# The scan's 64x64 products on four tiles of TensorE instead of two, in a hybrid attention and RWKV-7 encoder

## The chip, the cores and the metric

The kernel runs on one core of a Trainium2 chip. The metric is the device time of one execution in microseconds. The kernel before took 3055.45 us, the median of three runs (3053.56 to 3060.9).

## The reference

One encoder layer is applied to two sequences, of 1024 and 256 tokens, with model width 1024. The layer normalises the tokens, projects them once, and sends the columns to two groups of heads:

- four heads of differential attention (width 512), and
- eight heads of bidirectional RWKV-7 time mixing (width 512, head size 64).

Both results are joined, projected by `w_out` and added to the input. Then come 16 SwiGLU experts that each choose their tokens, and a last norm. The part that matters here is the time mixing. For each head, and once in each direction of time, it runs

```
def step(S, inp):
    r_t, w_t, k_t, v_t, a_t, b_t = inp
    Sa = jnp.einsum('bhij,bhj->bhi', S, a_t)
    S = S * w_t[:, :, None, :] + Sa[..., None] * b_t[:, :, None, :] + v_t[..., None] * k_t[:, :, None, :]
    y = jnp.einsum('bhij,bhj->bhi', S, r_t)
    return S, y
...
y = ys[0] + ys[1]
mean = jnp.mean(y, axis=-1, keepdims=True)
var = jnp.mean((y - mean) ** 2, axis=-1, keepdims=True)
y = ((y - mean) * lax.rsqrt(var + GN_EPS)).reshape(B, T, RWKV_WIDTH) * lnx_w + lnx_b
...
return ((y + bonus) * g)
```

with a state S of 64x64 per head. Everything is fp32 at the interface.

## The kernel before, in words

The kernel is a row of blocks, each closed before the next one opens: norm and projection, attention, the scan, the group norm of the scan's result, the output projection with the router, the experts, the last norm. Features go between blocks through the DRAM tensor `feat` (40 tiles of 128 x 1280).

**The scan** (L754 to L1150) works in chunks of C = 64 tokens. One step g takes 128 tokens, two chunks, of all eight heads and of both directions d (direction 1 runs from the end). There are NG = 10 steps, eight for the long sequence and two for the short one. Two heads lie in one tile of 128 partitions, head 0 of the pair on partitions 0 to 63 and head 1 on 64 to 127, and there are RT = 4 such tiles f. An array for a step has NI = 8 items i (4 tiles by 2 chunks) of 64 columns. All products are 64x64 times 64x32, 64x64 or 64x128 in fp32.

PE's work is written out by hand, and each group ends with a semaphore. `heads(out, lhsT, rhs)` (L895 to L898) issues two products, one for each partition half: rows 0 to 63 into output partitions 0 to 63, rows 64 to 127 into 64 to 127. These are the diagonal tiles of the 128x128 array. `turned` (L900 to L903) transposes in the same way, by a product with the identity. PSUM has eight banks of 512 columns; direction d owns four of them, `at_bank(d, b, i)` with b from 0 to 3.

A step of PE is, in this order:

1. *pairs*: `bt` and then `kt` against `ar`, 128 columns each, for both directions, into banks 0/1 and 2/3.
2. the first transpose, of `invT`, into bank 0.
3. *levels* l = 1 to 5, which double the size of the block in which a triangular matrix is inverted. Each level has `ax` for both directions (bank 0), then at levels 2 to 4 the transposes of one of three token arrays for both directions (bank 3, the table TOKENS), then `xax` for both directions: up to two calls per item, into banks 1 and 2.
4. the *scan half* c = 0 and 1: G (bank 3), u (bank 0), and y with the state's update (banks 1 and 2), for both directions each.

The other engines follow by semaphores. ACT copies PSUM to SBUF after each group (L998, L1002, L1006, L1011, L1014) and computes the decays of the next step behind c = 0. DVE masks the pairs (L1078, L1081, L1069), adds each level's result to `inv` and `invT` (L1094, L1096), and adds y and the state (L1109 to L1123). Between these it does the next step's preparation: `rates` after levels 2 to 4 (L1042 to L1048), `running` before the y of c = 0 (L1033, L1035), and `blocks` before the y of c = 1 (L1056 to L1061). Each of these stands at a fixed place in DVE's program. POOL multiplies the masked pairs with the ten level masks of a step (L883), level 1 of both directions first, then levels 2 to 5 of direction 0, then those of direction 1. PE waits for each of them with `lvl_masked`.

The block behind the scan loads `bonus`, `gate` and `w_out` (L1183 to L1188), sums heads with a matrix of ones (L1206), and norms and gates the result `yacc`. ACT and POOL meanwhile split `w_out` into two halves of 16 bits.

Lines that the prediction names beside these: L1576 is a product of the experts in f16, on the full array.

Of the kernel before, what the change touches and what calls it, by code (L numbers as in the profile page):

```python
# [8 lines left out]
P = 128  # L9
D = 1024  # L10
KD = D // P
# [5 lines left out]
RW = 512  # L17
RT = RW // P
# [4 lines left out]
C = 64  # L23
# [30 lines left out]
def build(nc, tokens, gains, sub_g, w_in, lam_qk, par, w2, a2, g2, w_out, w_router,  # L54
# [12 lines left out]
    with ExitStack() as ctx:  # L67
# [785 lines left out]
        with nc.Block() as block:  # L853
# [33 lines left out]
            @block.tensor  # L887
            def _(pe):
                H = (slice(0, C), slice(C, 2 * C))

                def at_bank(d, b, i, w=C):
                    o = (4 * d + b) * 512 + i * w
                    return ps[:, o:o + w]

                def heads(out, lhsT, rhs, start=True, stop=True):  # L895
                    for h in H:
                        ins = pe.matmul(out[h], lhsT[h], rhs[h], start=start, stop=stop)  # L897
                    return ins  # L898

                def turned(out, lhsT):  # L900
                    for h in H:
                        ins = pe.matmul(out[h], lhsT[h], ident[h, h], start=True, stop=True)
                    return ins  # L903

                def step(g):
                    par = g % 2
                    for b, x in ((0, bt), (2, kt)):
                        for d in range(2):
                            if b == 0:
                                pe.wait_ge(bd_ready[d], g + 1)  # L910
                                if g:
                                    pe.wait_ge(y_read[d], 2 * g)
                            for i in range(NI):
                                ins = heads(at_bank(d, b + i // 4, i % 4, 2 * C), x[d][:, i],
                                            ar[d][par][:, i].rearrange("p a b -> p (a b)"))
                            ins.then_inc(pairs_psum[d], 1)
                    for d in range(2):
                        pe.wait_ge(masks_ready[d], 3 * g + 2)
                        for i in range(NI):
                            ins = turned(at_bank(d, 0, i), invT[d][:, i])  # L920
                        ins.then_inc(first_psum[d], 1)
                    for l in range(1, NL + 1):
                        for d in range(2):
                            pe.wait_ge(inv_ready[d], NL * g + l)
                            pe.wait_ge(lvl_masked[d], NL * g + l)
                            for i in range(NI):
                                ins = heads(packed(at_bank(d, 0, i, C // 2), l), alv[d][:, l - 1, i],
                                            half_of(inv[d][:, i], l, d == 1))
                            ins.then_inc(ax_psum[d], 1)
                        for dt, q in TOKENS.get(l, ()):  # L930
                            if q == 0:
                                pe.wait_ge(masks_ready[dt], 3 * g + 3)
                                pe.wait_ge(vb_in[dt], 16 * g + 16)
                            else:
                                pe.wait_ge(tok_read[dt], NTOK * g + q)
                            x = (vb, bt, kt)[q][dt]
                            for i in range(NI):
                                ins = turned(at_bank(dt, 3, i), x[:, i])
                            ins.then_inc(tok_psum[dt], 1)
                        for d in range(2):  # L940
                            pe.wait_ge(prod_ready[d], NPR * g + l)
                            if l == 1:
                                pe.wait_ge(masks_ready[d], 3 * g + 3)
                            for i in range(NI):
                                x = prod(d, l)[:, i]
                                if l < NL:
                                    heads(packed(at_bank(d, 1, i, C // 2), l), invT[d][:, i], half_of(x, l, d == 1))
                                ins = heads(packed(at_bank(d, 2, i, C // 2), l), x, half_of(invT[d][:, i], l, d == 0))
                            ins.then_inc(xax_psum[d], 1)
                    for c in range(2):  # L950
                        for d in range(2):
                            pe.wait_ge(state_ready[d], 2 * g + c + 1)
                            if c == 0:
                                pe.wait_ge(tok_read[d], NTOK * (g + 1))
                            for f in range(RT):
                                i = 2 * f + place(d, c)
                                heads(at_bank(d, 3, f), ar[d][par][:, i, 0], state[d][:, f], stop=False)
                                ins = heads(at_bank(d, 3, f), km[d][:, i, 0], tokv[d][:, i], start=False)
                            ins.then_inc(g_psum[d], 1)
                        for d in range(2):  # L960
                            pe.wait_ge(prod_ready[d], NPR * g + NL + 2 * c + 1)
                            if c == 0:
                                pe.wait_ge(invT_final[d], g + 1)
                            for f in range(RT):
                                ins = heads(at_bank(d, 0, f), invT[d][:, 2 * f + place(d, c)], gu[d][:, f])
# [12 lines left out]

                for g in range(NG):
                    step(g)  # L980
# [45 lines left out]
            def _(v):  # L1026
# [47 lines left out]
                def step(g):  # L1074
                    more = g + 1 < NG
                    for d in range(2):
                        v.wait_ge(pairs_psum[d], 2 * g + 1)
                        v.tensor_tensor(inv[d], pair_banks(d, 0).rearrange("p (a w b) -> p a w b", w=2, b=C)[:, :, 0],  # L1078
                                        lvl[:, d, 0:1, :].broadcast_to([P, NI, C]), ALU.mult)
                        v.drain()  # L1080
                        v.tensor_tensor(invT[d], inv[d], ident2[:, :].unsqueeze(1).broadcast_to([P, NI, C]),  # L1081
                                        ALU.add)
                        v.drain().then_inc(masks_ready[d], 1)
                    for d in range(2):
                        mask_pairs(d, bm, 0)
                    for d in range(2):
                        v.wait_ge(pairs_psum[d], 2 * g + 2)
# [92 lines left out]
        with nc.Block() as block:  # L1180
            @block.sync
            def _(sp):
                sp.dma_start(bonus, feat[F_BONUS:F_BONUS + RT].rearrange("t p n -> p t n")).then_inc(post_in, 16)  # L1183
                sp.dma_start(gate, feat[F_GATE:F_GATE + RT].rearrange("t p n -> p t n")).then_inc(post_in, 16)

                sp.dma_start(wo_raw, w_out.rearrange("(k p) n -> p k n", p=P)).then_inc(wo_in, 16)
                sp.dma_start(wr, w_router.rearrange("(k p) n -> p k n", p=P)).then_inc(wo_in, 16)
                sp.dma_start(g2n, gains[1:2, :].partition_broadcast(P)).then_inc(wo_in, 16)  # L1188
                for b in range(2):
# [1 line left out]

            @block.gpsimd
            def _(pool):
                pool.wait_ge(post_in, 32)
# [23 lines left out]
            def _(act):  # L1218
                for f in range(RT):
# [6 lines left out]
                                   scale=1.0 / 64).then_inc(std_ready, 1)  # L1226

                    if f == 0:
                        act.wait_ge(wo_in, 48)
# [8 lines left out]
            def _(v):  # L1238
# [5 lines left out]
                                           ALU.mult, ALU.add).then_inc(centred, 1)  # L1244

                centre(0)
                v.wait_ge(post_in, 32)
                for f in range(RT):
                    if f + 1 < RT:
                        centre(f + 1)  # L1250
# [43 lines left out]
        with nc.Block() as block:  # L1294
# [33 lines left out]
            @block.tensor  # L1328
            def _(pe):
                pe.drain().then_inc(out_psum, 2)  # L1330
                pe.wait_ge(wo_in, 48)

                def project(t, b, half):
                    for k in range(KD):
# [78 lines left out]
            def _(v):  # L1413
                for b in range(2):
                    v.drain().then_inc(h6_stored[b], 16)
                v.wait_ge(wo_in, 48)
# [444 lines left out]
```

## Time and profile before

| | |
|---|---|
| median of three runs | 3055.45 us |
| profiled execution, its own time | 3056.16 us |
| its span, first to last instruction | 3054.3 us |
| PE busy over the span | 2750.1 us (90%) |
| weight loads (PEld) | 2130.6 us (70%) |
| DVE | 1995.9 us (65%) |
| ACT | 1438.8 us (47%) |
| POOL | 321.0 us (11%) |
| the scan's stretch, 743 to 1325 us | 582.0 us |
| PE busy in it | 573.9 us |

An engine's busy time is the time in which at least one of its instructions is in work, so overlapping products on PE count once. PEld is the same engine loading weights beside its products. A share over the whole span is an average over blocks with different limits; the scan is best read by itself. In a timeline a row is a run of instructions of one line, with its start, its length, its count and the idle time before it.

### The profile page before, as it was taken

The page shows a single profiled execution, that of the slowest core. Times are in us where ns is not written, and L with a number is a line of the kernel's source. Part 1 is how long each engine was busy: PE and PEld are TensorE (multiplying, and loading weights), DVE is VectorE, ACT ScalarE, POOL GpSimd, SP SyncE. Part 2 cuts the span into 40 slices and gives each one's busy share as a digit, 9 for nine tenths or more (in the row PEclk, how much of TensorE's full clock was granted, in tenths as well). Part 3 has the DMA queues.
Part 4 walks back from the last instruction along what each step waited for, and adds up shares of the span by engine and source line. Part 5 has one row for each costly group of instructions (what it writes and reads, how often), then busy time and mean ns, then how long its engine had stood idle before and what let it go on. Part 6 is the DMA issues. An engine that isn't in the chain of part 4 may idle for free. (4 is left out here: it accounts for less than half of the span.)

```text
span 3054.3 us, 90989 instructions
## 1 busy us (share of the span) xinstructions
PE 2750.1 (90%) x39070; PEld 2130.6 (70%) x39070; DVE 1995.9 (65%) x3188; ACT 1438.8 (47%) x2171; POOL 321.0 (11%) x260
## 2 busy tenths in 40 slices
PE   5999988996999999955934999999999999999994
PEld 3455544665999999942524777888877777788872
DVE  3344077776565455434268888888888888888883
ACT  3211155664222222222223666666666666666663
POOL 0000000002113112213200100111111000011000
PEclk8999999997999999977966999999999999999997
DMA  4113141002112112033315999999999999999984
GB/s 129 34 37 142 27 193 67 0 0 77 52 51 74 52 45 80 11 147 110 124 41 203 308 307 333 312 311 318 309 316 308 309 300 314 320 319 309 315 278 154
DMA packets 282900, 544.78 MB, mean 178 GB/s; under 512 B 13296, under 2 KB 96880, under 8 KB 282576
## 3 DMA queue, kind: packets, MB, share of 16 engines
q1 hardware_dynamic: 273728, 505.62, 48.1%
q0 software_dynamic: 8848, 34.08, 4.3%
q8 instruction: 296, 4.85, 0.6%
q14 instruction: 28, 0.23, 0.0%
HBM read 487.23 MB, written 52.43 MB: 177 GB/s over the span
## 5 line engine op out<-in xcount | busy, mean ns | idle before, releaser
L1677 DVE SCALAR_TENSOR_TENSOR arena<-arena 128x1024 f16<-128x1024 f32 x768 | 904.2, 1221 | 95.2 <-ACT arena L1622 95.0
L1576 PE MATMUL ps<-arena 128*128 128x160 f16 x12288 | 854.4, 233 | 8.2 <-DVE arena L1686 3.3
L1576 PEld LDWEIGHTS ps<-arena 128*128 128x128 f16 x12288 | 850.8, 98 | 12.8 <-issue 9.6
L1622 ACT ACTIVATE arena<-arena 128x1024 f16<-128x1024 f32 x768 | 766.7, 1049 | 145.3 <-PE ps L1601 144.9
L897 PE MATMUL ps<-arena 64*64 64x32 f32 (+2 forms) x14080 | 501.5, 224 | 22.4 <-DVEq L1062 21.2
L897 PEld LDWEIGHTS ps<-arena 64*64 64x64 f32 x14080 | 481.5, 135 | 28.5 <-DVEq L1062 21.4
L1593 PE MATMUL ps<-arena 128*128 128x512 f16 x1536 | 363.6, 388 | 0.0
L389 PE MATMUL ps<-arena 128*128 128x512 f16 (+1 forms) x1584 | 285.7, 344 | 0.7 <-ACT arena L235 0.7
L1593 PEld LDWEIGHTS ps<-arena 128*128 128x128 f16 x1536 | 142.3, 99 | 182.8 <-issue 36.4
L389 PEld LDWEIGHTS ps<-arena 128*128 128x128 f16 x1584 | 154.9, 98 | 131.7 <-ACT arena L235 1.2
L1643 ACT ACTIVATE arena<-ps 128x160 f32<-128x160 f32 x256 | 77.7, 304 | 256.8 <-PE ps L1576 256.6
L883 POOL TENSOR_TENSOR arena<-arena,lvl 128x512 f32<-128x512 f32 x100 | 123.8, 1273 | 429.8 <-DVEq L1072 429.1
L1094 DVE TENSOR_TENSOR arena<-arena,ps 128x256 f32<-128x256 f32 x80 | 33.8, 422 | 184.8 <-PE ps L897 184.8
L307 DVE SCALAR_TENSOR_TENSOR arena<-arena 128x1024 f16<-128x1024 f32 x22 | 26.9, 1225 | 181.2 <-ACT arena L240 181.2
L600 PE MATMUL ps<-arena 128*128 x288 | 126.1, 582 | 17.6 <-DVEq L695 15.3
L1705 DVE SCALAR_TENSOR_TENSOR arena<-ps,arena 128x160 f32<-128x160 f32 x256 | 82.5, 322 | 79.1 <-ACT arena L1643 77.6
L1002 ACT COPY arena<-ps 128x256 f32<-128x256 f32 x100 | 37.7, 377 | 203.7 <-PE ps L897 203.7
L1336 PE MATMUL ps<-arena 128*128 128x512 f16 x480 | 109.4, 386 | 24.2 <-POOL arena L1326 24.2
L240 ACT ACTIVATE arena<-arena 128x1024 f16<-128x1024 f32 x22 | 23.1, 1056 | 217.5 <-PE ps L389 217.5
L1528 POOL TENSOR_TENSOR carry<-carry 1x1 f32<-1x1 f32 x16 | 2.9, 183 | 1127.1 <-ACT arena L1660 1127.1
L651 ACT ACTIVATE arena<-arena 128x1024 f32<-128x1024 f32 (+1 forms) x80 | 81.6, 1021 | 64.0 <-DVE arena L710 63.1
L1601 PEld LDWEIGHTS ps<-arena 128*32 128x32 f16 x3072 | 70.2, 96 | 55.4 <-issue 54.2
(219 smaller groups left out, 2911.0 us busy)
## 6 DMA issues: line engine op xcount, KB each, us to landing
arena<-w_gate SPq DMA_DIRECT2D x128, 1024.0 KB, 5.1
arena<-w_up SPq DMA_DIRECT2D x128, 1024.0 KB, 5.6
arena<-w_down SPq DMA_DIRECT2D x128, 1024.0 KB, 6.5
arena<-feat SPq DMA_DIRECT2D x120, 256.0 KB, 4.7
feat<-arena SPq DMA_DIRECT2D x20, 640.0 KB, 3.0
arena<-w_in SPq DMA_DIRECT2D x21, 512.0 KB, 3.9
arena<-tokens SPq DMA_DIRECT2D x20, 512.0 KB, 4.1
feat<-arena POOLq DMA_DIRECT2D x1, 7680.0 KB, 22.8
```

What stands on the lines that cost most here:

```text
L389: ins = pe.matmul(ps[:, b * 2048 + o:b * 2048 + o + c], wb2[:, b, w, k * P:(k + 1) * P], hT2[:, x, k, o:o + c], start=(k == 0 and n == 0), ...
L600: ins = pe.matmul(ps[:, m * T0 + o:m * T0 + o + w], qz[:, m, t0 + i * P:t0 + (i + 1) * P], qk[:, ds(h + HEADS_A, 1), t0 + o:t0 + o + w] .r ...
L651: act.activation(sc[:, u % 2, m, 0:n], sc[:, u % 2, m, 0:n], ACT.Exp, bias=srow[:, u % NR, m:m + 1], accum_out=srow[:, u % NR, 2 + m:3 + m ...
L883: pool.tensor_tensor(alv[d][:, l - 1], bm[d][:, :, 0], lvl[:, d, l:l + 1, :].broadcast_to([P, NI, C]), ALU.mult).then_inc(lvl_masked[d], 1)
L897: ins = pe.matmul(out[h], lhsT[h], rhs[h], start=start, stop=stop)
L1336: ins = pe.matmul(bank(2 * b + half), ot2[:, b, x, k], wo2[:, k, w, half * 512:(half + 1) * 512], start=(k == 0 and n == 0), stop=(k == KD ...
L1576: ins = pe.matmul(ps[:, o:o + SLOTS], part(4 * c + 2 * w + k // 4, pw) [:, k % 4, f * P:(f + 1) * P], xT2[:, px, k], start=(k == 0 and i = ...
L1593: pe.matmul(bank(2 + half), hid2[:, px, n, 0:CAP0], part(k, pw)[:, f, half * 512:(half + 1) * 512], start=first, stop=last)
L1622: act.activation(split[k % SPLIT][:, q * PW:(q + 1) * PW], ring[k % RING][:, q * PW:(q + 1) * PW], ACT.Copy, scale=W_SCALE).then_inc(w_hi, 1)
L1643: act.activation(sil[:, n % 2], ps[:, (n % 2) * 512:(n % 2) * 512 + SLOTS], ACT.Silu, scale=1.0 / W_SCALE).then_inc(silu_ready, 1)
L1677: v.scalar_tensor_tensor(split[k % SPLIT][:, WCH + q * PW:WCH + (q + 1) * PW], ring[k % RING][:, q * PW:(q + 1) * PW], W_SCALE, split[k % ...
L1705: v.scalar_tensor_tensor(h32[:, n % 2], ps[:, (n % 2) * 512 + SLOTS:(n % 2) * 512 + 2 * SLOTS], 1.0 / W_SCALE, sil[:, n % 2], ALU.mult, AL ...
```

## The change

Two new helpers issue the two products of a call on the other two tiles of the array: rows 0 to 63 into output partitions 64 to 127, and rows 64 to 127 into 0 to 63.

- The first transpose, all `ax`, the first call of each `xax` item (levels 1 to 4), all of G and u, and three of the five calls of y use the crossed helpers. The others stay on the diagonal.
- At levels 2 to 4 the token transposes alternate call by call with `ax` of the same level, instead of following both directions. Which direction and array a level has is unchanged. Their waits now stand ahead of the `ax` group that they alternate with.
- In y the two kinds alternate: crossed, diagonal, crossed, diagonal, crossed.
- What is written crossed lies on exchanged partition halves: `invT` (filled by two half operations of DVE instead of one), `gu` between G and u, and `yacc`. In DVE's program bm's mask for a direction now follows that direction's `invT` directly.
- Because `yacc` is exchanged, `bonus` and `gate` are loaded in halves that are exchanged (four DMAs of 64 partitions instead of two of 128), the rows of `w_out` that meet it too (three DMAs instead of one), and the two norm parameters are rolled on the host by 64.

```diff
+                def across(out, lhsT, rhs, start=True, stop=True):
+                    for h in range(2):
+                        ins = pe.matmul(out[H[1 - h]], lhsT[H[h]], rhs[H[h]], start=start, stop=stop)
+                    return ins
+
+                def turned_across(out, lhsT):
+                    for h in range(2):
+                        ins = pe.matmul(out[H[1 - h]], lhsT[H[h]], ident[H[h], H[h]], start=True, stop=True)
+                    return ins
...
-                            ins = turned(at_bank(d, 0, i), invT[d][:, i])
+                            ins = turned_across(at_bank(d, 0, i), invT[d][:, i])
...
+                            turn = TOKENS[l][d] if l in TOKENS else None
+                            if turn is not None:
+                                dt, q = turn
+                                if q == 0:
+                                    pe.wait_ge(masks_ready[dt], 3 * g + 3)
+                                    pe.wait_ge(vb_in[dt], 16 * g + 16)
+                                else:
+                                    pe.wait_ge(tok_read[dt], NTOK * g + q)
+                                x = (vb, bt, kt)[q][dt]
                             for i in range(NI):
-                                ins = heads(packed(at_bank(d, 0, i, C // 2), l), alv[d][:, l - 1, i],
-                                            half_of(inv[d][:, i], l, d == 1))
-                            ins.then_inc(ax_psum[d], 1)
-                        for dt, q in TOKENS.get(l, ()):
-                            ...
-                            for i in range(NI):
-                                ins = turned(at_bank(dt, 3, i), x[:, i])
-                            ins.then_inc(tok_psum[dt], 1)
+                                ins = across(packed(at_bank(d, 0, i, C // 2), l), alv[d][:, l - 1, i],
+                                             half_of(inv[d][:, i], l, d == 1))
+                                if i == NI - 1:
+                                    ins.then_inc(ax_psum[d], 1)
+                                if turn is not None:
+                                    ins = turned(at_bank(dt, 3, i), x[:, i])
+                            if turn is not None:
+                                ins.then_inc(tok_psum[dt], 1)
...
-                                    heads(packed(at_bank(d, 1, i, C // 2), l), invT[d][:, i], half_of(x, l, d == 1))
+                                    across(packed(at_bank(d, 1, i, C // 2), l), invT[d][:, i], half_of(x, l, d == 1))
                                 ins = heads(packed(at_bank(d, 2, i, C // 2), l), x, half_of(invT[d][:, i], l, d == 0))
...
-                                heads(at_bank(d, 1, f), state[d][:, f], ar[d][par][:, i, 1], stop=False)
-                                heads(at_bank(d, 1, f), tokv[d][:, i], km[d][:, i, 1], start=False, stop=False)
+                                across(at_bank(d, 1, f), state[d][:, f], ar[d][par][:, i, 1], stop=False)
                                 if f == 0:
                                     pe.wait_ge(prod_ready[d], NPR * g + NL + 2 * c + 2)
-                                heads(at_bank(d, 1, f), gu[d][:, f], bm[d][:, i, 1], start=False)
                                 heads(at_bank(d, 2, f), tokb[d][:, i], gu[d][:, f], stop=False)
-                                ins = heads(at_bank(d, 2, f), tokk[d][:, i], tokv[d][:, i], start=False)
+                                across(at_bank(d, 1, f), tokv[d][:, i], km[d][:, i, 1], start=False, stop=False)
+                                heads(at_bank(d, 2, f), tokk[d][:, i], tokv[d][:, i], start=False)
+                                ins = across(at_bank(d, 1, f), gu[d][:, f], bm[d][:, i, 1], start=False)
...
-                        v.tensor_tensor(invT[d], inv[d], ident2[:, :].unsqueeze(1).broadcast_to([P, NI, C]),
-                                        ALU.add)
+                        for h in range(2):
+                            src, dst = slice(C * h, C * h + C), slice(C - C * h, 2 * C - C * h)
+                            v.tensor_tensor(invT[d][dst], inv[d][src],
+                                            ident2[src, :].unsqueeze(1).broadcast_to([C, NI, C]), ALU.add)
                         v.drain().then_inc(masks_ready[d], 1)
-                    for d in range(2):
                         mask_pairs(d, bm, 0)
...
-                sp.dma_start(bonus, feat[F_BONUS:F_BONUS + RT].rearrange("t p n -> p t n")).then_inc(post_in, 16)
-                sp.dma_start(gate, feat[F_GATE:F_GATE + RT].rearrange("t p n -> p t n")).then_inc(post_in, 16)
-
-                sp.dma_start(wo_raw, w_out.rearrange("(k p) n -> p k n", p=P)).then_inc(wo_in, 16)
+                for h in range(2):
+                    src, dst = slice(C * h, C * h + C), slice(C - C * h, 2 * C - C * h)
+                    for x, t in ((bonus, F_BONUS), (gate, F_GATE)):
+                        sp.dma_start(x[dst], feat[t:t + RT, src].rearrange("t p n -> p t n")).then_inc(post_in, 16)
+
+                w_rows = w_out.rearrange("(k p) n -> p k n", p=P)
+                sp.dma_start(wo_raw[:, 0:RT], w_rows[:, 0:RT]).then_inc(wo_in, 16)
+                for h in range(2):
+                    src, dst = slice(C * h, C * h + C), slice(C - C * h, 2 * C - C * h)
+                    sp.dma_start(wo_raw[dst, RT:KD], w_rows[src, RT:KD]).then_inc(wo_in, 16)
```

G and u change `heads` to `across` in the same way. The waits for `post_in` go from 32 to 64 and those for `wo_in` from 48 to 80.

## Rows read from the trace of the kernel before

**Rows 1.** The page's head.
```profile
span 3054.3 us, 90989 instructions
```
**Rows 2.** Windows: stretch, length, each engine's busy time and count, clock, DMA.
```profile
743.00:1325.00 582.00, 573.88 (x17920) 566.26 (x17920) 312.32 (x585) 146.39 (x332) 123.79 (x100) 0.99 0.20 53
1325.00:1420.00 95.00, 33.00 (x67) 14.43 (x68) 50.62 (x16) 27.56 (x25) 34.48 (x16) 0.66 0.41 154
1330.00:1340.00 10.00, 6.01 (x12) 2.80 (x12) 0.00 (x0) 3.24 (x3) 0.00 (x0) 0.83 1.02 418
```
**Rows 3.** Groups by line, 743 to 1325: busy us, mean ns, idle before.
```profile
L897 PE MATMUL ps<-arena 64*64 64x32 f32 (+2 forms) x14080 | 501.5, 224 | 22.4 <-DVEq L1062 21.2 <-issue 0.7
L897 PEld LDWEIGHTS ps<-arena 64*64 64x64 f32 x14080 | 481.5, 135 | 28.5 <-DVEq L1062 21.4 <-issue 1.6
```
**Rows 4.** Waits, 743 to 1325: total us, times, longest.
```profile
DVE arena L1094 <- PE ps L897: 184.8, 80, 6.4
```
**Rows 5.** Line 1078: duration ns, first and last start us.
```profile
L1078 DVE TENSOR_TENSOR arena<-ps,lvl x20: 691/692/692, 747.1 to 1269.8; 128x512 f32<-128x512 f32 x20
```
**Rows 6.** Timeline of weight loads in one step: start, length, line.
```profile
878.07 5.88 PEld L897 LDWEIGHTS ps<-arena 64*64 64x64 f32 x192
883.82 2.00 PEld L902 LDWEIGHTS ps<-ident,arena 64*64 64x64 f32 x64
...
901.12 0.20 PEld L897 LDWEIGHTS ps<-state,arena 64*64 64x64 f32 x4
...
904.14 0.20 PEld L897 LDWEIGHTS ps<-arena,state 64*64 64x64 f32 x4
...
904.72 0.20 PEld L897 LDWEIGHTS ps<-arena,state 64*64 64x64 f32 x4
```
**Rows 7.** Timeline of DVE in the same step.
```profile
861.69 0.69 DVE L1078 TENSOR_TENSOR arena<-ps,lvl 128x512 f32<-128x512 f32 x1 [0.40 <-PE ps L897]
862.46 0.69 DVE L1081 TENSOR_TENSOR arena<-arena,ident 128x512 f32<-128x512 f32 x1
863.43 0.69 DVE L1078 TENSOR_TENSOR arena<-ps,lvl 128x512 f32<-128x512 f32 x1 [0.28 <-PE ps L897]
...
865.02 5.26 DVE L1069 TENSOR_TENSOR arena<-ps,causal 128x1024 f32<-128x1024 f32 x4
...
880.18 0.42 DVE L1094 TENSOR_TENSOR arena<-arena,ps 128x256 f32<-128x256 f32 x1 [4.99 <-PE ps L897]
...
882.05 0.42 DVE L1094 TENSOR_TENSOR arena<-arena,ps 128x256 f32<-128x256 f32 x1 [0.30 <-PE ps L897]
...
906.74 0.14 DVE L1109 COPY carry<-carry 1x1 f32<-1x1 f32 x1 [0.94 <-PE ps L897]
...
907.66 0.43 DVE L1123 TENSOR_TENSOR state<-state,eb 128x256 f32<-128x256 f32 x1
...
910.79 0.69 DVE L1056 SCALAR_TENSOR_TENSOR arena<-arena 128x512 f32<-128x512 f32 x1
911.40 0.68 DVE L1057 TENSOR_TENSOR arena<-arena 128x512 f32<-128x512 f32 x1
...
916.21 0.14 DVE L1109 COPY carry<-carry 1x1 f32<-1x1 f32 x1 [0.21 <-issue]
...
919.52 0.69 DVE L1078 TENSOR_TENSOR arena<-ps,lvl 128x512 f32<-128x512 f32 x1 [0.41 <-PE ps L897]
```
**Rows 8.** Window of line 1206 alone: PE, then PEld.
```profile
1325.30:1327.80 2.50, 2.39 (x6) 1.06 (x6) 1.00 0.58 102
```
**Rows 9.** Timeline of POOL in the same step.
```profile
866.35 12.45 POOL L883 TENSOR_TENSOR arena<-arena,lvl 128x512 f32<-128x512 f32 x10 [44.89 <-DVEq L1072]
```
**Rows 10.** Timeline behind the scan: DVE's wait for the loads.
```profile
1340.92 1.49 DVE L1243 SCALAR_TENSOR_TENSOR arena<-ps,arena 128x1280 f32<-128x1280 f32 x1 [11.60 <-DMA arena<-feat]
```
**Rows 11.** The page's costliest groups, in f16 on the full array.
```profile
L1576 PE MATMUL ps<-arena 128*128 128x160 f16 x12288 | 854.4, 233 | 8.2 <-DVE arena L1686 3.3
L1576 PEld LDWEIGHTS ps<-arena 128*128 128x128 f16 x12288 | 850.8, 98 | 12.8 <-issue 9.6
```

More of the change, by code:

```diff
@@ L925, in step @@
                             pe.wait_ge(lvl_masked[d], NL * g + l)
-                            for i in range(NI):
-                                ins = heads(packed(at_bank(d, 0, i, C // 2), l), alv[d][:, l - 1, i],
-                                            half_of(inv[d][:, i], l, d == 1))
-                            ins.then_inc(ax_psum[d], 1)
-                        for dt, q in TOKENS.get(l, ()):
[L931 to L936, printed above, removed]
-                            for i in range(NI):
-                                ins = turned(at_bank(dt, 3, i), x[:, i])
-                            ins.then_inc(tok_psum[dt], 1)
+                            turn = TOKENS[l][d] if l in TOKENS else None
[7 more added lines that the diff above has]
+                                x = (vb, bt, kt)[q][dt]
+                            for i in range(NI):
+                                ins = across(packed(at_bank(d, 0, i, C // 2), l), alv[d][:, l - 1, i],
[6 more added lines that the diff above has]
+                                ins.then_inc(tok_psum[dt], 1)
                         for d in range(2):
@@ L956, in step @@
                                 i = 2 * f + place(d, c)
-                                heads(at_bank(d, 3, f), ar[d][par][:, i, 0], state[d][:, f], stop=False)
-                                ins = heads(at_bank(d, 3, f), km[d][:, i, 0], tokv[d][:, i], start=False)
+                                across(at_bank(d, 3, f), ar[d][par][:, i, 0], state[d][:, f], stop=False)
+                                ins = across(at_bank(d, 3, f), km[d][:, i, 0], tokv[d][:, i], start=False)
                             ins.then_inc(g_psum[d], 1)
@@ L964, in step @@
                             for f in range(RT):
-                                ins = heads(at_bank(d, 0, f), invT[d][:, 2 * f + place(d, c)], gu[d][:, f])
+                                ins = across(at_bank(d, 0, f), invT[d][:, 2 * f + place(d, c)], gu[d][:, f])
                             ins.then_inc(u_psum[d], 1)
@@ L1193, in _ @@
             def _(pool):
-                pool.wait_ge(post_in, 32)
+                pool.wait_ge(post_in, 64)
                 for f in range(RT):
@@ L1228, in _ @@
                     if f == 0:
-                        act.wait_ge(wo_in, 48)
+                        act.wait_ge(wo_in, 80)
                     for k in (2 * f, 2 * f + 1):
@@ L1246, in _ @@
                 centre(0)
-                v.wait_ge(post_in, 32)
+                v.wait_ge(post_in, 64)
                 for f in range(RT):
@@ L1330, in _ @@
                 pe.drain().then_inc(out_psum, 2)
-                pe.wait_ge(wo_in, 48)
+                pe.wait_ge(wo_in, 80)
                 def project(t, b, half):
@@ L1415, in _ @@
                     v.drain().then_inc(h6_stored[b], 16)
-                v.wait_ge(wo_in, 48)
+                v.wait_ge(wo_in, 80)
                 with v.Fori(0, NTT // 2) as j:
@@ L1836 @@
     par = np.concatenate([tiles(x["shift_mu"][0], ZT)] + [tiles(x[k][0], RT) for k in ("w0", "a0")]
-                         + [tiles(x[k][0].reshape(1, RW), RT) for k in ("k_k", "k_a", "r_k", "lnx_w", "lnx_b")], axis=1)
+                         + [tiles(x[k][0].reshape(1, RW), RT) for k in ("k_k", "k_a", "r_k")]
+                         + [np.roll(tiles(x[k][0].reshape(1, RW), RT), C, axis=0) for k in ("lnx_w", "lnx_b")], axis=1)
     dist = np.abs(np.arange(P)[:, None] - (np.arange(BIAS_W)[None, :] - (T0 - P))).astype(np.float32)
```

## The prediction, made before the changed kernel was run

> **What bounds the kernel now.** I read the page's head first, then the busy time by stage: of the span of 3054.3 us [rows 1] the scan takes 582.0 us, with PE busy for 573.9 of it and DVE for 312.3, and the stage behind it, where the loads are re-cut, is the 95 us from 1325 on [rows 2]. Stages are closed blocks, so what the scan loses or gains moves the end one for one. Then the groups of the scan: the top one is PE at one helper line with 64x64 products in fp32 [rows 3]. The waits say that DVE waits for PE at one line alone for 184.8 us [rows 4], where PE itself is idle only 582.0-573.9 = 8 us [rows 2]. So PE's pace is the bound, at first.
>
> Below, a call is one `heads` or `across`: two products, one per partition half. Each product has two load and two matmul records, so a call is four of each. A step g takes, from first to last L1078 and less the 1.7 us between its two directions, (1269.8-747.1-1.7)/9 = 57.9 us [rows 5].
>
> Price of a call. In y, five calls per tile of 64x64 on 64 columns take 904.72-904.14 = 0.58 us: 117 ns each. In the levels, 192 load records (48 calls of 32 columns) take 883.82-878.07 = 5.75 us, 120 ns each, short idle included [rows 6]. Half the columns, same pace. With 128 columns, eight calls (L1078 of both directions, 863.43-861.69) take 1.74 us, 218 ns each [rows 7]. The full array in fp32 takes 2.39 us for 1280 columns, 1.87 ns a column [rows 8]; 16 products of 128 columns in 1.74 us are 0.85. So the two diagonal tiles already run side by side, and up to 64 columns a call costs 117 ns whatever its columns: two passes of 58.5 on the same pair of tiles.
>
> **The change, part by part.**
> *Alternation.* `across` uses rows h and columns 1-h, the two idle tiles. Calls that follow each other on different pairs can overlap; two on the same pair can't. Per step and at 117 ns or below there are 416 calls: 16 first transposes, 80 A·X (`ax`), 48 token transposes, 144 in `xax`, 128 in the scan half. Alternating afterwards are ax with tokens (levels 2 to 4, 96), xax levels 1 to 4 (128), and y (80, per f A H A H A, so four changes and one repeat). Not alternating: first transposes, ax at levels 1 and 5, xax at 5, all of G and u (112). No row shows two column tiles on the same rows. Bounds: 58.5 ns (all four tiles free) and 117 ns (nothing overlaps). I take 65: the second pass of a call must wait for its first, 58.5, and the next call starts with it, 6 ns for issue; it is near the low end because the two tiles that [rows 7, 8] do show lose nothing to each other. Blocks of 16 alternating calls: 1.04 us (before 1.87). One f of y: 4·65+117 = 377 ns (before 585). PE's work per step falls by 224·52+16·208 = 15 us. Most of the question is how much of that the others let through.
>
> *What is late next*, followed through the step whose L1078 is at 861.69 [rows 7].
> Head: invT becomes two instructions of half the partitions; L1078 to L1081 is 0.77 us, and a 128x512 operation of DVE without a drain behind it steps by 0.61 (910.79 to 911.40 [rows 7]). A half-partition form has no row; I price it as the whole one (bounds 0.3 and 0.7 each). Also bm's mask of direction 0 moves before direction 1's L1078. Direction 0: 862.46+0.61+0.81 = 863.88, mask ends 865.2. Direction 1: L1078 865.2, invT 865.97, mask 867.39, ready 868.72; before it was ready at 865.02+1.32+1.33 = 867.67. So the transpose of direction 1 starts 1.05 us late, at 868.72. Level 1's ax is 1.8 us as before and ends 871.5; xax gains: 2.1 us, ends 873.6 (before 874.2).
> POOL: its ten masks run 12.45 us back to back from 866.35 [rows 9], 1.24 apart. Level 2 of direction 1 is the seventh, ready at 875.13 now, and PE's block starts there at 875.28, so POOL is just hidden. POOL's second mask waits for direction 1's bm, so the seventh comes at 868.72+7.43 = 876.15, where PE could start at 874.7. New wait: 1.45 us.
> Levels 2 to 5: from the last product of a `xax` to L1094 are 0.27 us, to inv_ready 1.1. DVE then does a `rates` operation (L1042) for the next step: L1094 of direction 0 is at 880.18, that of direction 1 at 882.05 after 0.30 idle [rows 7]. It can't take direction 1 before 1.6 us after direction 0, so direction 1's inverse is ready 0.27+1.6+0.83 = 2.7 us after direction 0's xax ends, against 1.04 us of PE work there. A level is then 2.7+1.04+1.04 = 4.8 us (before 7.6; 0.06 is a seam). With xax 2 of direction 0 ending at 878.2, level 4's ends at 887.7, level 5 (2.7 and three blocks of 0.93, not alternating: 5.5) ends at 893.2. Before: G's first load at 901.12 [rows 6]. Saved up to there: 7.95 us.
> Scan half: G, u and ACT's two copies between are unchanged (3.0 us for c=0). y: 1.5 instead of 2.3 us, twice. DVE's `running` for the next step moves along with them. State of c=0 d=1 is ready 1.7 us behind y, at 900.95 (before just ahead of `blocks`, 910.79). Then DVE does `blocks`, 910.79 to 916.21 = 5.42 us [rows 7], and only then adds y of c=1; the next step's first products wait for y_read, 0.9 us behind L1109 (906.74 to 907.66 [rows 7]): 900.95+5.42+0.9 = 907.3. PE's y would be done at 906.1, so DVE takes 1.2 us of what PE gains. Before: 917.56 (2.0 ahead of the next L1078, 919.52 [rows 7]).
> A step saves 917.56-907.3 = 10.2 us, of 15 that PE's work falls by. The last step has no `blocks`: 11 us. Nine and one: 103 us. The step followed is as long as the mean (L1078 at 861.69 and 919.52, 57.8 beside 57.9 us [rows 7, 5]), so it stands for the others.
>
> *A page against it.* The Trainium skill (TensorE: Matmul & The Clock Gate, Part 3: Packing small matmuls) says a weight load overlaps matmuls in flight only when the row group differs. This case's trace speaks against the strict form: L1576's loads (850.8 us) and matmuls (854.4 us) of full 128 rows share the same stretch [rows 11]. By that rule an alternating call would gain nothing, and the sum would be the second rival below. The same section says, and the page TensorEngine Tiling (Array Packing), Key Properties, repeats, that distinct tiles load and multiply in parallel; no row here has such a pair.
>
> *Loads behind the scan.* bonus and gate come in four issues of 64 partitions instead of two, w_out in three instead of one; bytes are equal. SP's issues are 0.4 to 1.4 us and lie under the transfers; DVE waits for them until 1340.92, 11.6 us [rows 10]. At equal rate: 0. If halves of the partitions landed at half the rate, 15.5 us more (the block opens at 1325.4, they land at 1340.9). I take 0: the bytes set the time, as 418 GB/s on a full DMA share shows there [rows 2]. Rolled parameters, the swapped halves of yacc and the waits 64 and 80 cost nothing on the device.
>
> **Sum.** 3054.3-103 = 2951 us span; the run's own time is 1.9 above the span (3056.2), which gives 2953; the profiled run is 0.7 above the median of 3055.45, so 2952. With 58.5 ns a call: 0.2 us less at levels 2, 3 and 4 and 0.2 less in y, level 1 hidden under POOL: 8 us less, 2944.
>
> **Rivals.**
> 1. Half overlap: the two tiles on the same rows share a feed, a call costs about 90 ns. Blocks are 1.44 us. Level 1's loss stays under POOL; level 2's xax 0 ends 0.9 later, a level is 2.7+2.9 = 5.6 (0.8 more, twice), y is 0.4 longer, twice. A step saves 10.2-0.9-1.6-0.8 = 6.9 us: 2986 us. For it: a floor of 58.5 ns that isn't columns could be a load port. Against: the two tiles that run together now show no such sharing.
> 2. No overlap: the change doesn't do what it says, 117 ns stays. Left are +1.05 us of DVE head and about -0.35 from ax d1 no longer waiting at levels 2 to 4 (tokens lie between): +0.7·10 = 7 us, 3062, within noise.
> 3. Changing pairs costs, the other side: at each change the next tile's weight load can't hide. Its price is up to one load record, 135 ns [rows 3]; some 286 changes a step. If the exposed part is a third of it, 45 ns, that is 12.9+0.7 us a step: 3191 us. It turns slower than before by over 0.3% once a change exposes more than 1 ns on top of rival 2. For: the floor is set by loads. Against: loads of the next product already start under the matmuls, 850.8 beside 854.4 us [rows 11].
> 4. The clock: PE now idles 1.0, 1.45 and about three times 0.6 us a step and 1.2 at its end. The granted clock is 0.99 in the scan and 0.66 in the stage with PE busy 33 of 95 us [rows 2]. PE would be busy near 88%; if a tenth of the scan ran at half clock, +25 us: 2977, inside the range.
>
> **How the numbers follow.** Forecast 0.70 (with rival 4 in it), half overlap 0.09, none 0.11, costly change 0.10. 2952 is the likeliest; its own range is 2930 to 2985. The range for 8 in 10 takes in half overlap and an overlap worse than half: 2928 to 3008. Faster by over 0.3% (9 us, what a measurement of this kernel can tell): 0.80; within: 0.09; slower: 0.11 (costly change, and the loads at half rate on top of rival 2).
>
> **What would show it.** Right: L1078 to L1078 near 47 us; y's five calls in 0.38 us and an alternating block of 16 in 1.04; POOL as releaser of PE at level 2; DVE's idle before L1094 nearly gone; PE waiting for DVE at the step's end. G and u unchanged. DVE's L1243 wait still near 11.6 us. Wrong: blocks of 1.87 us (rival 2), longer (rival 3), steps below 44 us (DVE's half-partition operations or its chain cheaper than read), or the 95 us behind the scan longer.

## The result, and the profile after

The changed kernel takes 3087.1 us, the median of five runs (3080.0 to 3095.0), against 3055.45 us before. The ratio is 1.010, 95% interval 1.0075 to 1.0125: slower by 1%, where 3.4% faster was forecast. Its profiled execution took 3086.4 us.

Three marks cut both traces: the first masking operation of DVE in the scan (L1078, now L1092), the first product of the group norm behind it (L1206, now L1227), and the first product of the output projection (L1336, now L1357).

| us | before | after | forecast |
|---|---|---|---|
| scan, mark 1 to 2 | 578.3 | 585.3 | 475 |
| block behind it, mark 2 to 3 | 87.7 | 105.3 | 87.7 |
| all that follows | 1641.2 | 1647.0 | 1641.2 |

The last row is scatter: the same stretch takes 1644.3 us in e2 and 1649.6 in e4 below, which leave scan and experts as they were. The other two rows are the result.

The page of the kernel after: its span, the products' busy time, and the queue that carries instructions (packets, MB, share).
```profile
span 3084.5 us, 91013 instructions
PE 2651.0 (86%) x39070; PEld 2016.8 (65%) x39070; DVE 2013.2 (65%) x3208; ACT 1432.7 (46%) x2171; POOL 320.8 (10%) x260
q8 instruction: 296, 4.85, 0.6%
```
PE is busy 99 us less for the same 39070 matmul records, and the kernel is slower. So the tiles do overlap, and PE then stands idle. Windows of the kernel after answer [rows 2]: the scan, one alternating `xax` block of 64 matmul records, one idle stretch, and one block of 32 that does not alternate.
```profile
743.00:1332.00 589.00, 470.38 (x17920) 450.61 (x17920) 327.60 (x605) 140.58 (x332) 123.85 (x100) 0.89 0.20 52
869.30:870.23 0.93, 0.93 (x66) 0.93 (x65) 0.76 (x2) 0.00 (x0) 0.93 (x2) 1.00 0.00 0
871.10:873.00 1.90, 0.32 (x23) 0.21 (x13) 0.15 (x1) 0.37 (x1) 1.90 (x3) 1.00 0.00 0
909.26:910.20 0.94, 0.94 (x32) 0.94 (x34) 0.91 (x2) 0.10 (x1) 0.00 (x0) 1.00 0.00 0
```
Sixteen alternating calls take 0.93 us, 58 ns each, as the forecast's low end had it; eight that stay on one pair take 0.94, 117 ns each. The granted clock of the whole scan is 0.89, not 0.99. The waits of the kernel after, from 743 to 1360 us (total, times, longest), answer [rows 4]:
```profile
DVE arena L1109 <- PE ps L897: 168.2, 61, 6.4
PE ps L902 <- issue: 43.3, 37, 2.2
PE ps L897 <- issue: 27.8, 23, 2.0
PE ps L912 <- DVEq L1086: 17.6, 10, 1.9
PE ps L907 <- issue: 13.0, 12, 1.6
```
"Issue" is time in which PE waited for nothing that the profile shows; before it was under 2 us in the scan (0.7 in [rows 3]). PE's wait for DVE's mask at L1086 was forecast at 1.0 us a step; it is 1.8. In levels 2 to 4 the idle stretches come at one distance, whatever group they fall in. Three windows of PE there, each from one resumption to the next:
```profile
873.00:876.92 3.92, 2.29 (x127) 1.00 0.46 125
876.92:880.81 3.89, 2.30 (x127) 1.00 0.07 17
880.81:884.63 3.82, 2.15 (x128) 1.00 0.02 4
```
128 matmul records, with 128 loads 256 instructions, and then a pause until 3.8 to 3.9 us are over. The queue q8 moves 4.85 MB in 296 packets, 16 KB each; over 256 instructions that would be 64 bytes each. So the reading was: PE's program arrives in packets of 64 products, one per 3.85 us or so when PE is always hungry. A step has 1792 records, 14.0 packets, 53.9 us.

The queue's own rows bear this out. Of q8 the scan has (packets, MB, share), 743 to 1332 us:
```profile
q8 instruction: 140, 2.29, 1.6%
```
That is 14.0 packets a step. The three packets that began at 870.38, 874.34 and 878.05 us had landed at 871.76, 875.49 and 879.48; PE resumed at 873.01, 876.94 and 880.83, each time 1.25 to 1.45 us later. Over the scan, 61 of PE's 96 idle stretches of over 0.3 us end 1.2 to 1.55 us behind the landing of such a packet. The kernel before has the same 140 packets there, and its PE idles 8 us in all.

The step itself: DVE's line of mask operations answers [rows 5], and its timeline [rows 7].
```profile
L1092 DVE TENSOR_TENSOR arena<-ps,lvl x20: 691/692/693, 746.9 to 1278.0; 128x512 f32<-128x512 f32 x20
```
```profile
857.57 0.69 DVE L1092 TENSOR_TENSOR arena<-ps,lvl 128x512 f32<-128x512 f32 x1 [0.17 <-PE ps L897]
858.35 1.39 DVE L1097 TENSOR_TENSOR arena<-arena,ident 64x512 f32<-64x512 f32 x2
859.85 1.23 DVE L1083 TENSOR_TENSOR arena<-ps,causal 128x1024 f32<-128x1024 f32 x1
861.20 0.69 DVE L1092 TENSOR_TENSOR arena<-ps,lvl 128x512 f32<-128x512 f32 x1
861.97 1.73 DVE L1097 TENSOR_TENSOR arena<-arena,ident 64x512 f32<-64x512 f32 x2
863.82 3.91 DVE L1083 TENSOR_TENSOR arena<-ps,causal 128x1024 f32<-128x1024 f32 x3
```
(1278.0-746.9-3.6)/9 = 58.6 us a step, against 57.9; 3.6 us lie between the masks of the two directions. bm's mask of direction 1 starts 6.25 us behind L1092; 5.70 was forecast.

The block behind the scan answers [rows 2, 10]: one window (busy times, clock, DMA share, GB/s) and DVE's wait.
```profile
1350.00:1360.00 10.00, 0.00 (x0) 0.00 (x0) 0.00 (x0) 0.00 (x0) 0.00 (x0) 0.50 1.03 200
```
```profile
1360.81 1.49 DVE L1264 SCALAR_TENSOR_TENSOR arena<-ps,arena 128x1280 f32<-128x1280 f32 x1 [24.73 <-DMA arena<-feat]
```
The DMA engines are fully busy as before, at 200 GB/s instead of 418.

### The profile page after: what moved, and what is told of

It is laid out like the page before. It is cut to its first block and busy times, and to the rows that moved or that the text cites. A ratio compares the mean times of both kernels' runs of the same rounds, so it can differ in the third digit from the quotient of the medians.

```text
span 3084.5 us, 91013 instructions
## 1 busy us (share of the span) xinstructions
PE 2651.0 (86%) x39070; PEld 2016.8 (65%) x39070; DVE 2013.2 (65%) x3208; ACT 1432.7 (46%) x2171; POOL 320.8 (10%) x260
## 3 DMA queue, kind: packets, MB, share of 16 engines
q8 instruction: 296, 4.85, 0.6%
## 5 line engine op out<-in xcount | busy, mean ns | idle before, releaser
L902 PE MATMUL ps<-arena 64*64 64x32 f32 (+1 forms) x8320 | 352.6, 234 | 44.9 <-issue 43.3
L902 PEld LDWEIGHTS ps<-arena 64*64 64x64 f32 x8320 | 324.8, 152 | 52.9 <-issue 47.4
L897 PE MATMUL ps<-arena 64*64 64x32 f32 (+2 forms) x5760 | 263.5, 244 | 59.0 <-issue 27.8
L897 PEld LDWEIGHTS ps<-arena 64*64 64x64 f32 x5760 | 244.0, 146 | 63.7 <-issue 42.1
L600 PE MATMUL ps<-arena 128*128 x288 | 126.1, 582 | 17.6 <-DVEq L695 15.3
L1357 PE MATMUL ps<-arena 128*128 128x512 f16 x480 | 109.1, 385 | 23.7 <-POOL arena L1347 23.7
```

Source lines behind the costliest of these rows:

```text
L600: ins = pe.matmul(ps[:, m * T0 + o:m * T0 + o + w], qz[:, m, t0 + i * P:t0 + (i + 1) * P], qk[:, ds(h + HEADS_A, 1), t0 + o:t0 + o + w] .r ...
L902: ins = pe.matmul(out[H[1 - h]], lhsT[H[h]], rhs[H[h]], start=start, stop=stop)
L1357: ins = pe.matmul(bank(2 * b + half), ot2[:, b, x, k], wo2[:, k, w, half * 512:(half + 1) * 512], start=(k == 0 and n == 0), stop=(k == KD ...
```

## The experiments

Nine kernels ran. Scan and block are between the marks of the table above; the ratios of medians are against the kernel before on the same chip. e3, e4, e5 and e7 ran once: their totals have no interval, and what rests on them is read from their traces.

### The loads: e1_whole_loads and e2_half_loads_before

```
e1, from the kernel after (same for gate; w_out in one piece; waits 32 and 48)
- for h in range(2): ... sp.dma_start(x[dst], feat[t:t + RT, src]...)
+ sp.dma_start(bonus, feat[F_BONUS:F_BONUS + RT].rearrange("t p n -> p t n"))
e2, from the kernel before: the halved loads, with dst = src
```


> The changed kernel with bonus, gate and w_out loaded whole, as before (so the halves of the gated result and of w_out's rows are not exchanged, and the output differs). Theory A, loads of half the partitions are slow and make the block behind the scan longer: DVE's wait for the loads falls from 24.7 back to 11.6 us, first project product 88 us behind the scan's end instead of 105, total near 3070. Theory B, the block is longer for another reason (clock, ACT's order): total stays near 3087.

> The kernel before with only the loads of bonus, gate and w_out cut into halves of 64 partitions, each into its own half, nothing exchanged. If halves are the cost: +13 to +17 us, near 3070. If the exchange of halves (source rows of one half into the partitions of the other) is the cost: 3055 to 3057, no change.

Measured: e1 3072.0 us (ratio 1.0058, 1.0041 to 1.0075), block 86.5 us, scan 587.6. e2 3074.6 us (1.0063, 1.0046 to 1.008), block 105.1, scan 577.9. DVE's waits for the loads, e1 from the waits and e2 from the timeline, and a window of e2:
```profile
DVE arena L1258 <- DMA arena<-feat: 11.8, 1, 11.8
```
```profile
1351.44 1.49 DVE L1249 SCALAR_TENSOR_TENSOR arena<-ps,arena 128x1280 f32<-128x1280 f32 x1 [24.83 <-DMA arena<-feat]
```
```profile
1335.00:1345.00 10.00, 0.49 (x3) 0.08 (x1) 0.00 (x0) 0.00 (x0) 0.00 (x0) 0.79 1.03 206
```
The halves are the cost, not the exchange: loads into 64 partitions run at half the rate even with nothing exchanged. It is the whole of the 17.6 us. DVE's wait is 13 us of it. The block's length goes by ACT, whose first step on `w_out` waits for `w_out` and for the small loads queued behind it, `gains` last; it starts 46.1 us behind mark 2 in the kernel after (1378.26) and 27.9 before (1353.26).

### The supply of instructions: e4_pace and e3_fewer_transposes

e4 is the kernel before with a block of its own between scan and group norm; `same` is a diagonal call, `cross` a crossed one, each call into the next of the eight banks. A drain stands between the parts.
```
+ for n in range(160):
+     same(n, 64)
...
+ for n in range(160):
+     (cross if n % 2 else same)(n, 64)
...
+ for n in range(96):
+     (cross if n % 2 else same)(n, 128)
...
+ with pe.Fori(0, 20) as j:
+     for n in range(8): (cross if n % 2 else same)(n, 64)
```


> The kernel before with a block of PE alone between scan and group norm, no waits on others: 160 calls of 64 columns on the diagonal, 160 alternating, 96 alternating of 128 columns, and 160 alternating of 64 columns as a loop of 20 by 8 calls. Theory A (supply of 3.85 us for 32 calls): 18.7, then 17 to 20 with gaps of 1.9 us every 128 matmul records, then 10.5 to 11.5; the loop is 9.3 if its instructions stay on the engine and 18 or more if they are fetched again. Theory B (the gaps need DVE's and ACT's waits): 18.7, 9.3, 10.5, 9.3.

The four parts, and below them three resumptions of the second part (PE alone):
```profile
1321.80:1340.50 18.70, 18.66 (x639) 18.69 (x640) 0.00 (x0) 0.00 (x0) 0.00 (x0) 1.00 0.02 5
1340.80:1358.20 17.40, 10.26 (x627) 9.59 (x628) 0.00 (x0) 0.00 (x0) 0.00 (x0) 1.00 0.02 4
1358.50:1370.00 11.50, 11.23 (x390) 10.38 (x383) 0.00 (x0) 0.00 (x0) 0.00 (x0) 1.00 0.02 4
1370.50:1381.70 11.20, 11.15 (x639) 11.04 (x640) 0.00 (x0) 0.00 (x0) 0.00 (x0) 1.00 0.01 1
```
```profile
1343.16:1346.91 3.75, 2.09 (x128) 1.00 0.02 4
1346.91:1350.65 3.74, 2.09 (x128) 1.00 0.02 4
1350.65:1354.67 4.02, 2.09 (x128) 1.00 0.01 4
```
The same 160 alternating calls take 17.4 us as straight code, idle for 7.1 of them, and 11.2 us as a loop of 8 calls, with no idle stretch. Nothing else waits or is waited for in this block. Only where the instructions come from differs, so the pauses are instruction supply; theory B falls. The queue agrees (q8 in the second part, then in the loop, each for 1280 instructions):
```profile
q8 instruction: 4, 0.07, 1.5%
q8 instruction: 1, 0.02, 0.5%
```
(The second part's fifth packet began 0.4 us ahead of the window.) All five pauses of the second part end 1.3 to 1.5 us behind the landing of a packet. The diagonal calls, 18.7 us for 5 packets, already ran at the supply's pace: in its calls of up to 64 columns the kernel before had no slack that four tiles could use. (The loop's 70 ns a call, above 58, was not followed up.)

e3 takes instructions out of the changed kernel: only the last of eight token transposes is issued, and ACT writes zeros for the tokens.
```
- if turn is not None:
+ if turn is not None and i == NI - 1:
```


> The changed kernel with one token transpose of eight at each place (84 of 832 products a step are left out) and ACT writing zeros for the tokens. Theory A, PE waits for its instructions, which come in packets of 16 KB (64 products in fp32) at 3.85 us each: 1.3 packets less a step, 5 us, the scan 50 us shorter, 3037. Theory B, the gaps come from the four tiles or from DVE's chain: the alternating transposes cost next to nothing, the scan is 0 to 10 us shorter, 3077 or above.

Measured: the scan 568.7 us, 16.6 shorter; 3128.6 us in all, since what follows the block took 1708 us (its tokens are zero; why that is slower was not followed up). In number it lies between the theories. The window shows what the forecast left out:
```profile
740.00:1313.00 573.00, 520.92 (x16240) 509.53 (x16240) 329.74 (x606) 140.65 (x332) 123.88 (x100) 0.76 0.20 53
```
The granted clock was 0.76, against 0.89. A step of e3 had 10 to 38 us at the low clock. A line through its nine step lengths against those times gives 50.9 us at full clock; the same through the 18 steps of the changed kernel and e1 gives 54.9 us, and 0.28 us more for each us at the low clock (correlation 0.84). So 4.0 us less for 1.31 packets, 3.1 a packet, on a fit (3.85 were expected); e4 is the clean proof.

### The clock: e7_idle_diagonal and e5_filled

e7 is the kernel before, diagonal tiles only, with PE made to wait.
```
+ if l < NL:
+     v.tensor_copy(km[d], km[d])
  v.drain().then_inc(inv_ready[d] if l < NL else invT_final[d], 1)
```


> The kernel before, diagonal tiles only, with one more DVE operation (km copied onto itself, 1024 columns, 0.6 to 1.2 us) ahead of each direction's inv_ready at levels 1 to 4, so that PE waits for DVE there: 3 to 8 us of PE idle a step in pieces of 1 us, and no gap of supply. If idle PE alone makes the clock fall, low stretches of 3.4 us and more appear in most steps and the scan's clock falls under 0.97. If the four tiles or the 1.8 us gaps are needed, the clock stays 0.99 and steps grow by the idle time alone.

e5 is e1 with work that nobody reads put into each `xax` group.
```
+ def fill(d):
+     across(ps[:, 4 * d * 512 + 256:4 * d * 512 + 512], ident2, restart[:, 0:256])
...
  x = prod(d, l)[:, i]
+ if i in (1, 4, 6):
+     fill(d)
```


> The run with whole loads (e1_whole_loads), and in each of the ten xax groups of a step three more crossed calls of 256 columns into columns of PSUM that nobody reads: 0.43 us of PE work each in 8 instructions, so 240 instructions a step more. If PE's idle stretches are what makes the granted clock fall in the scan, the clock there rises from 0.88 towards 0.97 and the low stretches (10 to 20 us a step) fall under 5 us; supply then sets the step at about 15 packets by 3.85 = 58 us, even from step to step. If the clock falls for another reason (four tiles at work), it stays near 0.88 or falls, and steps grow to 62 us or more.

The scan of e7, then that of e1 and that of e5:
```profile
743.00:1415.00 672.00, 637.67 (x17885) 628.28 (x17884) 362.14 (x659) 146.36 (x332) 132.78 (x100) 0.89 0.17 45
```
```profile
740.00:1331.00 591.00, 481.70 (x17920) 461.52 (x17920) 327.18 (x606) 140.52 (x332) 123.91 (x100) 0.87 0.20 52
```
```profile
743.00:1358.00 615.00, 535.77 (x19120) 491.49 (x19120) 327.99 (x605) 140.66 (x332) 123.87 (x100) 0.98 0.19 50
```
PE's new wait in e7 (total, times, longest):
```profile
PE ps L897 <- DVEq L1099: 26.3, 38, 0.8
```
e7: PE idles 3.5 us a step instead of 0.7, in pieces of at most 0.8 us, and the clock falls to 0.89, with 10 to 17 us a step at 1.2 GHz where the kernel before had 3.4 us in nine steps; a step is 65 to 68 us. So neither four tiles nor supply gaps are needed for the fall: waits for DVE bring it too. A line through e7's nine steps gives 60.7 us at full clock and 0.45 us more for each us at the low clock. e5: with work in the gaps the clock is back at 0.98 (low stretches in three of nine steps), and steps are 60 to 63 us; 58 was expected, so filling cost 3 us more than its packets.

How much PE idles does not decide the clock by itself. PE still idles about 8 us a step in e5 and 1 to 5 in v2 below, both at 0.98, and 3.5 in e7 at 0.89; e3 idles 3 to 8 us at 0.76. The filling calls are also of 256 columns among calls of 32, so e5 changed more than the gaps. What made the difference stays open.

### DVE's head: e6_split_invT_before

```
- v.tensor_tensor(invT[d], inv[d], ident2[:, :].unsqueeze(1)..., ALU.add)
+ for h in range(2):
+     half = slice(C * h, C * h + C)
+     v.tensor_tensor(invT[d][half], inv[d][half], ident2[half, :].unsqueeze(1)..., ALU.add)
  v.drain().then_inc(masks_ready[d], 1)
- for d in range(2):
  mask_pairs(d, bm, 0)
```


> The kernel before with invT filled by two half operations of DVE (nothing exchanged) and bm's mask of a direction right behind it, as the change has it. By the prediction's working the transpose of direction 1 starts 1.05 us later in each step, +10 us, 3067; if half operations are no cheaper than read off the changed kernel (bm's mask of direction 1 is 6.25 us behind L1078 there, 5.70 forecast) +1.6 us a step, 3073. If the later start is caught up inside the step, as POOL's and DVE's waits there have slack, no change.

Measured: 3073.7 us (1.0062, 1.0045 to 1.0079), scan 593.5 us against 578.3: 1.5 us a step. Nothing inside the step catches it up. So the half operations and DVE's new order cost 15 us together, where PE has no slack.

### Two versions: v1_levels_only and v2_even_supply

v1 is the changed kernel with y as before (five `heads`), so that nothing is exchanged behind it and the loads are whole.

> Crossed products only from the first transpose to u; y on the diagonal as before, so yacc, the loads and the norm's parameters are as before and the output is complete. Theory A (supply and clock set the scan, half loads the rest): scan within 6 us of the changed kernel's, block behind it as before, total 3062 to 3072. Theory B (y's alternation was what gained): scan 20 us longer than the changed kernel's, total 3090.

Measured: 3085.9 us (1.0093, 1.0076 to 1.011); block 86.8, scan 607.8 us. The scan is as B said, and A, the supply as it was put there, misses by 16 us: y's alternation was worth 22 us. The time went where y is. From the first product with the state to the next step's first mask v1 takes 19.3 us a step, the changed kernel 17.5, and PE idles 0.7 us of it instead of 2.0; the rest of the step is 41.5 and 41.2 us, with 10.0 and 9.6 us idle. The likely reason, argued and not shown: the supply runs somewhat ahead while G and u wait for ACT and DVE, so that y's time on one pair of tiles is PE's own, while in the levels PE waits for packets anyway. A step would then be a sum over stretches of the longer of the two, not the longer of two sums.

v2 starts from the kernel before and puts crossed work where few instructions do much.
```
  for i in range(NI):
      ins = heads(at_bank(d, i // 4, i % 4, 2 * C), bt[d][:, i], ...)     # pairs, 128 columns
      ...
+     ins = turned_across(at_bank(d, 3, i), vb[d][:, i])                  # was at level 2
...
+ across(at_bank(d, 3, f), km[d][:, i, 0], tokv[d][:, i], start=(f == 0), stop=False)   # ahead of state_ready
```


> From the kernel before: one token transpose group per direction crossed and put between the 128-column pairs, where few instructions do much work; kt pairs, km, tokv and tokk on exchanged halves; in the scan half the parts that need no new state are issued ahead of the waits. Loads as before. Theory A (supply): 1.9 us of transposes hidden in 3.5 us of pairs and 0.7 us of state wait hidden, at unchanged packets: step 55 to 56 us, total 3030 to 3040, granted clock in the scan stays 0.97 or more. Theory B (any alternation brings gaps and a falling clock): step 58 us or more, total 3055 or above.

Measured: 3041.7 us (3036.8 to 3047.6), ratio 0.9945 (0.9928 to 0.9961). It is the fastest of all: 0.5% below the kernel before, where the changed one is 1.0% above it. Scan 565.3 us (before 578.3), window of it:
```profile
740.00:1310.00 570.00, 536.56 (x17921) 525.43 (x17921) 312.70 (x586) 146.22 (x332) 123.75 (x100) 0.98 0.21 54
```
The clock held. Theory A has its direction right and is a little short in size: steps are 54.8 to 59.4 us, 56.9 in the mean, where 55 to 56 was expected, and the total is just above its 3030 to 3040. PE still idles 1 to 5 us in each step.

## Why the prediction was wrong

- *Price of a call.* Right, at its low end. 58.5 to 65 ns was forecast for alternating calls and 58 came; no run shows the 6 ns put on for issue. Four tiles overlap fully in fp32, two column tiles on the same rows included. Rivals 1, 2 and 3, which were all about this price, are wrong. The rule of the Trainium skill that was weighed (TensorE: Matmul & The Clock Gate, Part 3: a weight load overlaps matmuls in flight only where the row group differs) would have given rival 2. The trace of the kernel after does not agree: it has the tiles on the same rows that were missing, and they overlap, at 58 ns a call.
- *What is late next* is the step that failed. It followed DVE, POOL and ACT and took PE's instructions for free. A step of 47.6 us was forecast, 7.95 us of the gain in the levels; the supply alone sets 14 packets by 3.85, 53.9 us, and 58.6 was measured. The row was in view: half the columns at the same 117 ns was read as a floor of two passes on the tiles. Floor and supply happen to be within 3% of each other (117 ns a call, and 3.75 to 3.85 us for 32 calls), and either explains [rows 6].
- *The clock* was rival 4 at +25 us and inside the forecast. It is right in kind: 13 us a step at the low clock, by the fit 0.284·12.9 = 3.7 us a step, some 37 us over the scan. That waits of PE can bring such a fall, e7 shows, and with wide calls in the gaps it was gone (e5); so the supply's gaps are the likely cause here. The fit splits the 58.6 us measured into 54.9 and 3.7; that the two add up is no test of it.
- *DVE's head.* 1.05 us a step was forecast; e6 has 1.5. bm's mask of direction 1 was 0.55 us later than worked out: 0.43 of it since from the first half operation of direction 1 to that mask there are 1.85 us (861.97 to 863.82), not 1.42. How much of this shows in the changed kernel's step, beside the supply, no run says.
- *POOL's wait at level 2* is not among PE's waits in the kernel after; PE came later to that place, by its own pauses.
- *Loads behind the scan.* 0 was taken, with an upper bound of 15.5 us for half the rate. Half the rate it was, and 17.6 us, above that bound: the loads that DVE waits for landed 13.1 us later (28.6 us behind mark 2, before 15.5), w_out and what is queued behind it came late too, and ACT's first step on it 18.2 us later. The argument that the bytes set the time assumed a rate that rests on 128 partitions.
- *Sum.* Forecast -103; measured +7 in the scan, +17.6 behind it, +6 of scatter: 30 us between the profiled spans, 31.7 between the medians. Even with whole loads (e1) the change is 0.6% slower.

## What to carry to other kernels

Before making an engine's work shorter in straight code, count its instructions per us: here PE was fed 256 instructions, 64 products in fp32, per 3.75 us, and a floor that does not move with the size of the operands may be that supply. Put work that saves engine time next to instructions that do much each, as v2 does, and read the granted clock afterwards, since short waits of PE can lower it (e7) and need not (v2). Keep loads on all 128 partitions, or price a halved one at about twice its time.

## What the runs showed of the hardware that was not expected

- Straight code on PE is supplied at 3.74 to 4.02 us per 256 instructions, and PE resumes 1.3 to 1.5 us behind the landing of a packet; a loop of 8 calls (16 products) is not held up (e4).
- Four 64x64 tiles in fp32, two of them on the same rows, run fully beside each other: 58 ns a call against 117 at 64 columns; at 128 columns 96 alternating calls take 11.5 us, 120 ns each, where the diagonal has 218. (The 96 calls are three packets, so 120 ns may be the supply's pace and not the tiles'.)
- Loads from DRAM into 64 partitions move 200 to 210 GB/s with the DMA engines fully busy; into 128 partitions 418.
- Some 3.5 us of PE idle in a step of 68, in pieces of at most 0.8 us, go with a granted clock of 0.89 in the scan, before 0.99 (e7); 8 us a step of idle with wide calls put between go with 0.98 (e5).
- Two half operations of DVE (64x512) take 1.39 us together, 1.73 in the second direction; a whole one (128x512) 0.69.
